# Moving the due times that order the instruction queues of a transformer kernel

## The reference, cut to what matters

```
for l in range(2):                                  # DEPTH
    x = x + 0.5 * swiglu_ffn(x, ...)                # stages 0 and 3
    h = rms_norm(x, mix_norm[l])                    # stages 1 and 4
    y_a = diff_attention(rope(rms(aq)), rope(rms(ak)), av, lam, ...)
    y_b = chunk_attention(rms(bq), rms(bk), bv, rel_bias)
    y_c = retention(rope(cq), rope(ck), cv, cg, ...)
    x = x + (g0*(y_a@wa) + g1*(y_b@wb) + g2*(y_c@wc)) @ w_out
    x = x + 0.5 * swiglu_ffn(x, ...)                # stages 2 and 5
x = x + [dilated_attention | ssd_mixer | rglru_mixer](rmsnorm(x)) @ w_out_2   # stage 6
x = rmsnorm(x + swiglu_ffn(x, ...))                 # stage 7
# swiglu_ffn(x) = (silu(h @ w_gate) * (h @ w_up)) @ w_down, h = rms_norm(x); w_* are 1024x2816, 2816x1024
```

## Time and profile before

| | |
|---|---|
| median of 3 runs | 3204.72 us (3203.59 to 3205.60) |
| the profiled execution | 3205.60 us, its span 3203.5 us |
| PE busy | 3152.9 us, 98% |
| PEld, DVE, ACT busy | 2592.1, 2171.1, 1489.6 us (81%, 68%, 46%) |
| share of PE in the chain that ended last | 91% |
| granted TensorE clock, mean | 0.993 of full |

### The profile page before, as it was taken

The page is one execution under the profiler, slowest core; times in us unless marked ns, Lnnn a source line. Parts: engine busy times, 40 slices in busy tenths (PEclk is TensorE's granted clock), DMA queues, the critical chain, the costliest instruction groups (busy, mean ns, idle before and its releaser), DMA issues.

```text
span 3203.5 us, 37741 instructions
## 1 busy us (share of the span) xinstructions
PE 3152.9 (98%) x15170; PEld 2592.1 (81%) x15170; DVE 2171.1 (68%) x3452; ACT 1489.6 (46%) x2313; POOL 76.0 (2%) x153
## 2 busy tenths in 40 slices
PE   9999989999999999999999999999999999999998
PEld 7889867777888888888967777888889877788887
DVE  7685778745467656856787855457576767767656
ACT  5453546543344435534445654245353455545433
POOL 0000010100000000000010100000000100000000
PEclk9999999999999999999999999999999999999999
DMA  4322331322333224233232232342331544133231
GB/s 171 119 79 76 102 101 54 107 85 86 98 126 119 77 91 135 66 102 112 69 100 77 87 90 78 94 157 72 94 117 55 109 89 65 61 131 112 68 103 60
DMA packets 234335, 304.01 MB, mean 95 GB/s; under 512 B 11696, under 2 KB 180016, under 8 KB 234160
## 3 DMA queue, kind: packets, MB, share of 16 engines
q1 hardware_dynamic: 227408, 284.73, 30.1%
q0 software_dynamic: 6608, 16.79, 1.8%
q10 hardware_dynamic: 144, 0.10, 0.0%
HBM read 293.17 MB, written 2.10 MB: 92 GB/s over the span
## 4 chain that ended last, share of the span: by engine, by line
PE 91%; DVE 6%; ACT 1%; issue 1%; DMA 0%; POOL 0%; DVEq 0%; ACTq 0%
PE bank L592 28%; PE bank L604 15%; PE bank L597 15%; PE bank L606 12%; PE bank L599 12%; PE bank L1403 2%; PE bank L1051 1%; PE bank L1452 1%; PE bank L1436 1%; DVE k_wl L824 1%; PE bank L1688 1%; PE bank L1246 1%; ACT k_wh L806 1%; PE bank L1579 0%; DVE k_sc L841 0%
## 5 line engine op out<-in xcount | busy, mean ns | idle before, releaser
L824 DVE TENSOR_TENSOR k_wl<-k_raw,k_wh 128x1024 fp32r<-128x1024 f32 (+1 forms) x314 | 368.8, 1175 | 343.4 <-ACT k_wh L806 342.1
L806 ACT ACTIVATE k_wh<-k_raw 128x1024 fp32r<-128x1024 f32 (+1 forms) x314 | 319.8, 1019 | 454.8 <-PE bank L604 301.6
L806 ACT ACTIVATE k_wh<-k_xraw 128x1024 fp32r<-128x1024 f32 (+1 forms) x279 | 277.3, 994 | 421.2 <-PE bank L604 197.0
L824 DVE TENSOR_TENSOR k_wl<-k_xraw,k_wh 128x1024 fp32r<-128x1024 f32 (+1 forms) x279 | 318.2, 1141 | 184.6 <-ACT k_wh L806 184.0
L592 PE MATMUL bank<-k_xh,k_wh 128*128 128x512 f32 x840 | 358.8, 427 | 0.0
L604 PE MATMUL bank<-k_xh,k_wl 128*128 128x512 f32 x840 | 330.3, 393 | 0.0
L597 PE MATMUL bank<-k_xl,k_wh 128*128 128x512 f32 x840 | 329.7, 393 | 0.0
L592 PE MATMUL bank<-k_h,k_wh 128*128 128x512 f32 x696 | 271.8, 391 | 0.0
L604 PE MATMUL bank<-k_h,k_wl 128*128 128x512 f32 x696 | 271.1, 390 | 0.0
L597 PE MATMUL bank<-k_h,k_wh 128*128 128x512 f32 x696 | 271.0, 389 | 0.0
L592 PE MATMUL bank<-k_wh,k_S 128*128 128x512 f32 (+1 forms) x656 | 246.5, 376 | 0.0
(11 more groups left out here) (377 smaller groups left out, 6622.1 us busy)
## 6 DMA issues: line engine op xcount, KB each, us to landing
k_raw<-in_w_in SPq DMA_DIRECT2D x153, 512.0 KB, 3.7
k_xraw<-in_ffn_w_gate SPq DMA_DIRECT2D x51, 512.0 KB, 4.4
k_xraw<-in_ffn_w_down SPq DMA_DIRECT2D x47, 512.0 KB, 4.6
k_xraw<-in_ffn_w_up SPq DMA_DIRECT2D x45, 512.0 KB, 4.6
k_raw<-in_w_out SPq DMA_DIRECT2D x28, 512.0 KB, 3.3
k_xraw<-in_ffn_w_gate SPq DMA_DIRECT2D x26, 384.0 KB, 3.3
k_raw<-in_ffn_w_down SPq DMA_DIRECT2D x26, 384.0 KB, 3.0
k_raw<-in_ffn_w_up SPq DMA_DIRECT2D x19, 512.0 KB, 4.4
```

The lines of the kernel that those rows point to most:

```text
L806: e.activation(self.pair[c.pair][0][:, 0:n], self.unit[c.src][:, 0:n], ACT.Copy).then_inc(*self.act.up(("wh", c.i)))
L824: e.tensor_tensor(lo[:, 0:n], self.unit[c.src][:, 0:n], hi[:, 0:n].bitcast(F32), ALU.subtract).then_inc(*self.dve.up(*marks))
```

## The change

No operation is added or removed, no wait, no buffer and no transfer. Some sixty due times get other values, and with them the order in which the instructions of one engine stand. The pieces of it that matter here:

```diff
 (dve_weights, the sums and differences of weight chunks)
-                yield c.split + 6.6
+                yield c.split + 0.6
 (pe_ffn_norm)
-        yield self.at[st]["start"] + (12.5 if st else 24.3)
+        yield self.at[st]["start"] + (12.5 if st else 20.5)
 (ffn_sums_ticks)
-        t = self.at[st][0, "B12"] + 6.4 + 9.8 * q
+        t = self.at[st][0, "B12"] + 1.0 + 9.0 * q
-                "S4": self.at[st][1, "P1"] + 5.5 + 4 * q}
+                "S4": self.at[st][1, "P1"] + 2.5 + 4 * q}
 (turn_tick)
-        return (self.at[st][0, "B22"] + 30.0 if b == 0 else self.at[st][b, "P3"] + 18.0) + 3.0 * q
+        return (self.at[st][0, "B22"] + 30.0 if b == 0 else self.at[st][b, "P3"] + 12.0) + 3.0 * q
 (pe_mixer_norm)
-        yield self.at[st]["start"] + 9.0
+        yield self.at[st]["start"] + 4.5
 (pe_qk, act_qk, dve_qk)
-            yield t + (6.0 if job[0] == "a" else 3.4)
+            yield t + (9.0 if job[0] == "a" else 6.0)
-                yield t + (10.1 if job[0] == "a" else 7.2)
+                yield t + (10.5 if job[0] == "a" else 7.2)
-                yield t + 0.0
+                yield t + 0.8
 (attention: kinds a, b and m2)
-            start, end = at["start"] + 98.0, at["phase2"] - 25.4
+            start, end = at["start"] + 86.0, at["phase2"] - 28.0
-            start, end = at["phase2"] - 14.0, at["phase3"] - 1.4
+            start, end = at["phase2"] - 14.0, at["phase3"] - 1.0
-        start, end = at["start"] + 58.6, at["xbc"][1].at + 8.0
+        start, end = at["start"] + 56.0, at["xbc"][1].at + 8.0
 (dve_retention)
-                yield t["score", j, kt] + 0.0
+                yield t["score", j, kt] + 1.5
 (dve_m2_z)
-            yield t + 0.0
+            yield t + 1.2
 (act_lru, the tanh)
-        yield t + 7.5
+        yield t + 10.5
 (ssd_ticks, dve_ssd_setup)
-        out.update({("state", c): u + 10.0 + 5.3 * c for c in range(3)})
+        out.update({("state", c): u + 10.0 + 4.5 * c for c in range(3)})
-            yield t["state", c] - 7.0
+            yield t["state", c] - 1.0
...
```

More of the change, by code:

```diff
@@ L965, in dve_ffn_sums @@
             e.tensor_tensor(half(d, i), half(self.X[j], 0), half(self.X[j], 1), ALU.subtract).then_inc(*self.dve.up(("sd", st, j)))
-        yield t["S3"] + 0.5
+        yield t["S3"] + 0.3
         rests("S3", s)
@@ L1092, in act_blocks @@
             for m in range(2):
-                yield self.done_at(st, b, "P2", m) + 2.3
+                yield self.done_at(st, b, "P2", m) + 1.5
                 e.wait_ge(*self.dve.sig(("d2", st, b, m)))
@@ L1149, in dve_downs @@
             for m in range(KD):
-                yield self.down_tick(st, part, m) + 0.0
+                yield self.down_tick(st, part, m) + 0.4
                 bank = self.p.group[st, "down", part, 0, m // 2 * 2].banks[m % 2]
@@ L1377, in act_halves @@
         for t, (q, k, ql, kl, qh, kh) in enumerate(a["q"]):
-            yield a["start"] + (8 * t - 5.0 if t else -2.5) * a["step"]
+            yield a["start"] + (8 * t - 8.0 if t else -2.5) * a["step"]
             for ref in a["ready"][t]:
@@ L1390, in dve_halves @@
         for t, (q, k, ql, kl, qh, kh) in enumerate(a["q"]):
-            yield a["start"] + (8 * t - 4.5 if t else -2.0) * a["step"]
+            yield a["start"] + (8 * t - 7.5 if t else -2.0) * a["step"]
             e.wait_ge(*self.act.sig(("kh", st, kind, t)))
@@ L1437, in pe_attention @@
                 j.then_inc(*self.pe.up(("turned", st, kind, x)))
-            yield a["start"] + (i + 0.2) * a["step"]
+            yield a["start"] + (i + 0.6) * a["step"]
             x = i - 6
@@ L1473, in dve_attention @@
         for i in range(38):
-            yield a["start"] + (i + 0.0) * a["step"]
+            yield a["start"] + (i + 0.2) * a["step"]
             x = i - 3
@@ L1490, in dve_attention @@
                 continue
-            yield a["start"] + (i + 0.2) * a["step"]
+            yield a["start"] + (i + 0.4) * a["step"]
             for x in (i - 1, i):
@@ L1517, in act_attention @@
         for i in range(38):
-            yield a["start"] + (i + 0.0) * a["step"]
+            yield a["start"] + (i + 0.5) * a["step"]
             x = i - 2
@@ L1576, in pe_heads @@
         for m, t, t2, b, s, r, mm_, y, gain in self.heads(st, kind):
-            yield t + 3.2
+            yield t + 4.0
             e.wait_ge(*self.act.sig(("hsq", st, kind, m)))
@@ L1596, in act_heads @@
         self.act_rstd(e, r, self.bank[b], 1.0 / P, 0, ("hrstd", st, kind, m))
-        yield t2 + 3.1
+        yield t2 + 1.0
         e.wait_ge(*self.dve.sig(("hn", st, kind, m)))
@@ L1603, in dve_heads @@
         _, t, t2, b, s, r, mm_, y, gain = self.heads(st, kind)[m]
-        yield t + 5.7
+        yield t + 6.5
         e.wait_ge(*self.act.sig(("hrstd", st, kind, m)))
@@ L1701, in act_gates @@
                 for m in range(2):
-                    yield done_tick(g, m) + 1.2
+                    yield done_tick(g, m) + 0.4
                     e.wait_ge(*self.pe.sig(("done", st, ("g", i, j), m)))
@@ L1745, in act_c @@
             for m in range(2):
-                yield done_tick(g, m) + 0.0
+                yield done_tick(g, m) + 0.4
                 e.wait_ge(*self.pe.sig(("done", st, job, m)))
@@ L1923, in act_lru @@
             e.activation(g, r, ACT.Tanh, scale=nsp[:, m:m + 1]).then_inc(*self.act.up(("th", st, m)))
-        yield t + 12.8
+        yield t + 12.0
         for m in two:
@@ L1928, in act_lru @@
             e.activation(a, r, ACT.Exp, scale=sp[:, m:m + 1]).then_inc(*self.act.up(("a", st, m)))
-        yield t + 15.7
+        yield t + 15.0
         for m in two:
@@ L1936, in act_lru @@
             r, g, a = self.lru_tiles(m)
-            yield t + 23.0 + 3 * (m % 2)
+            yield t + 20.0 + 3 * (m % 2)
             e.wait_ge(*self.dve.sig(("lru", st, m)))
@@ L2013, in pe_steps @@
         b = self.bank[7]
-        yield t + 9.5
+        yield t + 11.0
         e.wait_ge(*self.dve.sig(("out", st, "dt", 0)))
@@ L2020, in pe_steps @@
         i.then_inc(*self.pe.up(("dtT", st)))
-        yield t + 23.1
+        yield t + 22.0
         e.wait_ge(*self.dve.sig(("dta", st)))
@@ L2071, in ssd_ticks @@
         u = done_tick(x[3], 1)
-        out = {("xdt", c): t + 7.6 + 3 * c for c in range(4)}
-        out.update({("bc", g): u + 6.0 + 3.0 * g for g in range(2)})
-        out.update({("state", c): u + 10.0 + 5.3 * c for c in range(3)})
+        out = {("xdt", c): t + 8.0 + 3 * c for c in range(4)}
+        out.update({("bc", g): u + 6.0 + 1.5 * g for g in range(2)})
+        out.update({("state", c): u + 10.0 + 4.5 * c for c in range(3)})
         out.update({("head", q): u + 32.0 + 10.0 * q for q in range(4)})
@@ L2176, in pe_ssd_heads @@
                 L, C = self.ssd_tiles(h)
-                yield t["head", q] + 9.0 + 1.2 * j
+                yield t["head", q] + 9.0 + 0.8 * j
                 o, base = self.bank[6 + q % 2], 64 * j
@@ L2270, in dve_ssd_norm @@
         e.tensor_tensor(self.SC[8], self.SC[8], self.SC[9], ALU.add).then_inc(*self.dve.up(("ysq", st, g)))
-        yield t + 0.0
+        yield t + 2.5
         e.wait_ge(*self.act.sig(("srstd", st, g)))
@@ L2280, in dve_ssd_norm @@
             m = 2 * g + j
-            yield t + 5.3 + j
+            yield t + 4.5 + j
             y = self.Y2[self.y2(2, m)]
@@ L2293, in dve_m2_out @@
                 if part == 2:
-                    yield done_tick(g, m % 2) + 2.2
+                    yield done_tick(g, m % 2) + 1.8
                     self.dve_entry(e, st + 1, m)
```

## The result

The changed kernel takes 3308.15 us (median of 4 runs, 3305.27 to 3312.91), the kernel before 3204.15 us beside it: the ratio is 1.0326, with a 95% interval of 1.0310 to 1.0343. It is 104 us slower. I had forecast slower, 3236 us with a range of 3211 to 3268. The sign was right; the size was three times what I had.

The account below looks back on a forecast made before the run. PE, busy 98% of the span, was taken as the bound. Terms 20.5 + 1.8 + 7.8 - 4.3 + 3 + 2.9 = +31.7 us on the profiled 3205.6 gave 3237, forecast as 3236 us at the median; range 3211 to 3268.

Parts of the forecast that it names:

- Transposes and weight sums (+20.5): Five FFNs: a weight sum lands before L1135, h comes late, PE waits; 4.1 us an FFN, +20.5 us.
- The rest of the FFN edits I cost at 0: FFNs: activation sums, stage 0 norm, residuals and SiLU cost 0, several ticks remaining until PE asks.
- Norm (+1.8 in stage 6): Head of each mixer: L1187 moved 4.5 ticks earlier makes PE wait 1.8 us; counted whole in stage 6.
- aq and ak (+7.8 over two stages): Stages 1 and 4: DVE sets the pace and finishes later, 3.9 us each, +7.8 us, between 0 and +12.
- its three causes: At aq/ak: L824 awaiting a late chunk, 0.85 us; later first sum, 1.9; L824 ahead of last L1281, 1.13.
- Attention a (-4.3): Stages 1 and 4: 126 ticks instead of 116.6 cut waits and clock loss; -4.3 us for both, -8.6 to +4.
- Retention (+3): Mixers: L1659 stands up to two instructions further back, delaying PE's score groups; +3 us over two stages.
- Stage 6 (+2.9): Stage 6: L2142 places +0.85 and +1.4, L1861 +2.1, tanh behind SiLU saves 1.5 us; sum +2.9.
- A: Rival: DVE is ahead in the FFNs, so their term is 0 to 5 us; 3218 us, chance 0.13.
- B: Rival: faster, aq/ak not prolonged, longer attention removes maxima waits and clock losses, no FFN waits; 3189 us, chance 0.07.
- C: Rival: gains in the mixers cancel the FFN losses; no change, 3205 us, chance 0.10.
- D: Rival: queue locks, pieces standing before their input drag weights, or waits drop the clock; +30 us, 3266, chance 0.17.

Follow-up runs that it names:

- experiment 8: The kernel before with norm, aq/ak/bq/bk, step shifts, attention window, transposes and weight sums edited, plus heads, SiLU, residuals and recurrence: 3299.47 us.
- experiment 9: The kernel before with late ak L1281s, attention's DVE pieces and av's first L1344 earlier, last two ak rotations later: 3196.03 us, ratio 0.9968.
- experiments 2 (the first) and 7: Both against the kernel before: transposes at 12 ticks plus the norm's sum at 4.5, 3208.92 us; all edits no other experiment has, 3220.03 us.

## Why the prediction was wrong, point by point

**Transposes and weight sums (+20.5): right.** 4.02 to 4.07 us an FFN against 4.1, with 20 waits of L1051 for L1138, none with either edit alone. The working from four instructions of DVE and one of PE held to 0.1 us a block.

**"The rest of the FFN edits I cost at 0": wrong, about +1.5 us an FFN.** 1.1 us of it is the activation sums, by way of L606's wait for ACT's L1081. The reason given was "several ticks until PE asks for it", which I had looked up for the sums themselves, but not for L1081, which came to stand behind them on ACT.

**Norm (+1.8 in stage 6): right.** 1.9 us alone. In the changed kernel PE's wait is 2.6 us and the place costs 2.9; that the later residuals (L1150) add the 1 us fits, as the kernel with the heads and L1150 also has 2.6 and the one without has 1.7.

**aq and ak (+7.8 over two stages): right,** 3.8 and 4.6 us, norm included, and with its three causes in the trace. Two of its signs did not come: PE's wait for L1281 is in two pieces (2.8 and 3.5 us in stage 1) and not near 8, and the waits of L1246 went from 8.6 to 7.7 us and not to nothing, with one of 2.6 us in each mixer. But the same edits move bq and bk, which the forecast did not look at: 4.9 and 3.7 us. That is the first missed term.

**Attention a (-4.3): this is the step that failed.** It priced the longer window alone, and as a gain ("126 ticks instead of 116.6"), and "Nothing moves the weights L824, behind which a maximum can still stand" was half of what happened: the weights stayed, and the maxima moved behind them. Not priced at all were the shifts inside a step, nor the heads. The window measured +4.1 and +5.6 us, the shifts +9.8 and +10.6, and the heads on top of them about 6.5 and 3.9. With bq and bk, that is 49 us where I had -4.3, so 53 of the 74 us between the sum of the forecast (31.7) and the difference of the two profiled runs (105.7). The rest of the 74 is mostly in the FFNs and in stage 6. The mechanism is the one that I used in the FFN and did not use here: a small piece whose due time slides past a large one of the same queue.

**Retention (+3): wrong,** nothing at its ticks; what stands near it is the gates' and half a us. **Stage 6 (+2.9): mis-sized,** 9.5 us besides the norm's place; alone, the shifts inside a step cost 2.8 there. The first two places that I named came (L2114 waits 1.2 us, L1895 for L1861 1.0 us), but the large ones are the waits for L1831, where nothing had been, and L1874. The 2.3 us wait for L1508 that was to stay is gone. How much each is worth stays open, as told above.

**The rivals.** A and B fell with the FFN windows. C fell. D named the right family (a piece ahead of its input on an in-order queue, and more clock drops), but I priced only the drops, at 30 us. That price was not far off: the busy time that PE gained in the three mixers is 7.7 + 11.4 + 2.6 = 21.7 us. The larger part, 55 us there, is PE idle behind pieces that stand late in their queues, where the forecast had 11 us for the three mixers in all. The range ended with the price of the drops alone, at 3268, and so did not hold 3308. The Trainium skill ("TensorE: Matmul & The Clock Gate", part 1) has the clock fall to half after idleness; here it did so behind some of the new waits and not behind others (last section). The prediction took from it that the new short waits cost their length alone; this case does not bear that out, as the clock fell behind waits of 2.6 us and, in the kernel before, of 1.9 us.

## What to carry to other kernels

Where each queue is ordered by due times, an edit of a due time costs nothing until it crosses another piece of the same queue, and then it can cost up to that piece's whole duration, less the time for which nobody asked for the result (a sum of 0.95 us cost 0.53 at block 3). So list for every shifted piece which others it overtakes on its own engine, and for every wait it has whether the piece it waits for still comes first on the other. A piece that takes 0.3 us can cost 6 when it slides behind 4 us of work. Price the edits that look smallest (0.2 of a step) with the same care as the large ones, and do so together: two edits that cost 0.3 and 0.4 us alone cost 4 us a stage together, and edits that cost 1 to 2 us a mixer alone cost 4 to 6.5 on top of others.

## What was not expected of the hardware

The half clock behind a wait does not go by the wait's length alone. In the changed kernel PE waited 2.58 us for the norm and went on at full clock; behind a wait of 2.56 us for L1263, in the same stage, the clock was 0.72, and behind the 4.80 us wait for the maxima of pair 25 it was 0.56. PE's waits, then the windows behind them:

```profile
374.43 1.12 PE L1187 MATMUL bank<-k_acc,k_const 128*128 128x512 f32 x2 [2.58 <-DVE k_acc L889]
...
415.98 1.12 PE L1246 MATMUL bank<-k_sc,k_const 128*128 128x512 f32 x2 [2.56 <-ACT k_sc L1263]
...
552.39 0.58 PE L1403 MATMUL bank<-k_qkh 64*128 64x256 f32 x2 [4.80 <-DVE k_sm L1508]
```

```profile
374.40:380.00 5.60, 5.58 (x23) 4.28 (x24) 2.96 (x4) 2.38 (x3) 0.00 (x0) 1.00 0.17 60
416.00:422.00 6.00, 6.00 (x17) 4.25 (x17) 5.93 (x9) 3.34 (x5) 0.91 (x2) 0.72 0.50 131
552.40:558.00 5.60, 5.60 (x20) 4.46 (x21) 2.96 (x8) 2.18 (x5) 0.00 (x0) 0.56 0.29 93
```

It does not go by the place either. The kernel with the heads (experiment 8) has the same wait at the same norm, with a drop behind it:

```profile
374.92 2.07 PE L1187 MATMUL bank<-k_acc,k_const 128*128 128x512 f32 x2 [2.61 <-DVE k_acc L889]
```

```profile
374.90:380.50 5.60, 5.58 (x17) 3.84 (x18) 2.01 (x3) 2.23 (x3) 0.00 (x0) 0.74 0.16 57
```

It has one behind each of its three norms, the changed kernel behind none. What decides it, these runs do not show.

The wait at pair 17, tick 674, is 1.8 us long in the fast kernel of experiment 9 with no drop behind it, where 1.9 us at the same place had one in the profiled run of before:

```profile
499.15 0.39 PE L1403 MATMUL bank<-k_qkh 64*128 64x256 f32 x2 [1.79 <-DVE k_sm L1508]
```

```profile
499.50:504.00 4.50, 4.50 (x25) 3.46 (x22) 4.33 (x8) 4.16 (x10) 0.00 (x0) 1.00 0.02 4
```

By ticks that drop is worth 1.5 us, and the kernels of experiments 2 (the first) and 7, with the maxima where they were before, did not have it in stage 1. So the bonus of 1.7 us a stage that I credited to the attention for ending it was one that the kernel before did not always pay.
